# Ends of stages in a three-block fp32 network on one core: table loads ahead of waits, the second block's sum before the first's end, low parts by GpSimd

## The reference

```python
def _swiglu(t, w_gate, w_up, w_down):
    return (silu(t @ w_gate) * (t @ w_up)) @ w_down
# block 1, two layers
f = _swiglu(_rmsnorm(h, ffn1_pre_g[l]), ...)
h = h + 0.5 * _rmsnorm(f, ffn1_post_g[l])
u = _rmsnorm(h, mix_pre_g[l])            # -> three kinds of attention
h = h + _rmsnorm(merged @ w_out[l], mix_post_g[l])
f = _swiglu(_rmsnorm(h, ffn2_pre_g[l]), ...)
h = h + 0.5 * _rmsnorm(f, ffn2_post_g[l])
# stick-breaking attention, one of the three
log_beta = log_sigmoid(z); log_not = where(mask, log_beta - z, 0)
w = where(mask, exp(log_beta + reversed_cumsum(log_not) - log_not), 0)
# block 2, layers 0 and 1: ffn, mixer (sgu or rwkv), ffn
x = layer_norm(DN_ALPHA * x + 0.5 * swiglu(x, w_in, w_out), g, b)
x = layer_norm(DN_ALPHA * x + mix, g, b)
# block 3, one layer: attentions, convolution, hgrn; then
x = layer_norm_3(DEEPNORM_ALPHA * x + mixed, ln1_g, ln1_b)
ff = square(relu(x @ w_ff1)) @ w_ff2
```

## Time and profile before

| | us |
|---|---|
| median of three runs (lowest, highest) | 3549.11 (3548.95, 3560.91) |
| the profiled execution's own time | 3548.89 |
| its span in the trace | 3547.1 |
| PE busy | 3217.7 |
| DVE busy | 1777.1 |
| ACT busy | 1483.4 |
| POOL busy | 166.1 |
| mean granted TensorE clock, share of full | 0.92 |

### The profile page before, as it was taken

One profiled execution on the slowest core, in us unless ns is written; L12 is line 12 of the kernel. 1 busy time (PEld: TensorE's weight loads), 2 busy tenths in 40 slices (PEclk: granted clock), 3 DMA queues, 4 the chain that ended last, 5 costly groups with the idle time before them and its releaser, 6 DMA issues.

```text
span 3547.1 us, 54473 instructions
## 1 busy us (share of the span) xinstructions
PE 3217.7 (91%) x23904; PEld 2928.2 (83%) x23904; DVE 1777.1 (50%) x2137; ACT 1483.4 (42%) x1843; POOL 166.1 (5%) x210
## 2 busy tenths in 40 slices
PE   6999798999999798999998999998798998776798
PEld 6989787998988788989997898997597997655687
DVE  4554444545554435555543545446655543444655
ACT  4454734444454734444453344444303443321244
POOL 0000100000000100000000000000000000502100
PEclk9999888999999889999997999999798997867799
DMA  5543223554543224555551455553102453300253
GB/s 214 185 167 122 92 108 120 190 179 175 181 155 131 93 86 151 182 190 181 188 178 48 154 186 178 182 184 135 51 4 76 169 185 127 110 21 28 83 184 137
DMA packets 68591, 488.67 MB, mean 138 GB/s; under 512 B 7723, under 2 KB 9147, under 8 KB 9605
## 3 DMA queue, kind: packets, MB, share of 16 engines
q1 hardware_dynamic: 63936, 464.94, 36.8%
q10 hardware_dynamic: 4420, 20.26, 1.6%
HBM read 484.11 MB, written 1.06 MB: 137 GB/s over the span
## 4 chain that ended last, share of the span: by engine, by line
PE 79%; DVE 9%; ACT 8%; issue 2%; POOL 1%; PEld 1%; DMA 1%; DVEq 0%; ACTq 0%; PEldq 0%; SPq 0%; POOLq 0%
PE bank L100 52%; PE acc L100 26%; DVE weights_lo L315 2%; ACT weights_hi L110 2%; PEld acc L100 1%; ACT L1109 1%; ACT act_gate L640 1%; DVE h L652 1%; POOL hgrn_pairs_q L2913 0%; DVE h L663 0%; PE bank L683 0%; DVE xn L1670 0%; PE acc L968 0%; DVE b_x_lo L496 0%; ACT b_x_hi L110 0%
## 5 line engine op out<-in xcount | busy, mean ns | idle before, releaser
L315 DVE TENSOR_TENSOR weights_lo<-weight_ring,weights_hi 128x2048 fp32r<-128x2048 f32 x440 | 1009.8, 2295 | 1034.4 <-ACT weights_hi L110 1033.9
L100 PE MATMUL bank<-b_x_hi,weights_hi 128*128 128x256 f32 x3880 | 1102.9, 284 | 15.3 <-DVE weights_lo L315 6.4
L100 PE MATMUL bank<-b_x_hi,weights_lo 128*128 128x256 f32 x3880 | 1099.1, 283 | 0.0
L100 PE MATMUL bank<-b_x_lo,weights_hi 128*128 128x256 f32 x3880 | 1098.0, 283 | 0.0
L110 ACT ACTIVATE weights_hi<-weight_ring 128x2048 fp32r<-128x2048 f32 x440 | 839.6, 1908 | 436.9 <-PE acc L100 399.6
L100 PEld LDWEIGHTS bank<-b_x_hi,weights_hi 128*128 128x128 f32 x3880 | 739.2, 191 | 30.8 <-issue 15.5
L100 PEld LDWEIGHTS bank<-b_x_lo,weights_hi 128*128 128x128 f32 x3880 | 739.6, 191 | 3.2
L100 PEld LDWEIGHTS bank<-b_x_hi,weights_lo 128*128 128x128 f32 x3880 | 737.4, 190 | 0.0
L100 PE MATMUL acc<-weights_hi,b_hidden_hi 128*128 128x512 f32 x832 | 330.2, 397 | 0.0
L100 PE MATMUL acc<-weights_hi,b_hidden_lo 128*128 128x512 f32 x832 | 328.7, 395 | 0.0
L100 PE MATMUL acc<-weights_lo,b_hidden_hi 128*128 128x512 f32 x832 | 328.1, 394 | 0.0
(11 more groups left out here) (488 smaller groups left out, 4302.9 us busy)
## 6 DMA issues: line engine op xcount, KB each, us to landing
weight_ring<-in_weights SPq DMA_DIRECT2D x440, 1024.0 KB, 4.8
xn<-in_norm_rows ACTq DMA_DIRECT2D x15, 1024.0 KB, 4.7
bias_hankel<-bias_scratch ACTq DMA_DIRECT2D x1, 1536.0 KB, 6.2
cons<-in_shape_constants SPq DMA_DIRECT2D x1, 1408.0 KB, 6.8
h<-in_x SPq DMA_DIRECT2D x1, 1024.0 KB, 8.8
...
```

The costliest lines, as they stand in the source:

```text
L100: return pe.matmul(out, a, b, start=start, stop=stop, skip_group_check=True)
L315: dve.tensor_tensor(k.w.lo[:, n % 2, :], k.ring[:, n % RING, :], k.w.hi[:, n % 2, :], ALU.subtract) \
```

## The change

- `act_add_norm` and `act_residual` load the table with Sqrt first, ahead of their wait for the sum.
- In `act_add_norm` ACT squares the first half of block 1's sum without waiting for DVE's product by the gain; DVE waits for the squares instead.
- `dve_residual` does add 0, gain 0, add 1, norm 0, gain 1, norm 1; before, add 0, gain 0, norm 0, add 1, gain 1, norm 1.
- The low part of the unit behind an end is made by GpSimd (`pool_lo`), for 11 units: those behind `mixed` and `ffn2` of both layers, and the last units of f2(0,0), sgu, f2(0,2), f2(1,0), rwkv's output, f2(1,2) and block 3's output. Their mark is `w_lo_pool`, for which PE and SP wait. Behind `ffn1` DVE keeps it.
- `pe_features` runs a second warm behind `made` of block 1's first half in three places and none between the blocks; the transposes for `in2`, `h` "in" and `in3` stand ahead of their barriers, with 12 warm matmuls, each half with its own wait. `pe_h_features` is called for rwkv's output as well and gives it 12 warm matmuls too, where there were none.
- Scores of stick-breaking attention, the forget gates and hgrn load the set that holds Exp and Ln together ahead of their first wait. The compiled programs hold 114 table loads before and 85 now.

```diff
...
+EXP_AND_LN = "natural_log_exp_and_others"
...
 def unit(k, pe, *what, a=KT):
-    pe.wait_ge(*k.s.at("w_lo", n))
+    pe.wait_ge(*k.s.at(*low_mark(k, n)))
...
 def lo(k, dve):
+def lo_of_pool(k):
+    if k.s.counting:
+        k.by_pool.append(k.n_lo)
+    k.n_lo += 1
+def pool_lo(k, pool):
+    n = k.by_pool[k.n_pool]
+    k.n_pool += 1
+    pool.wait_ge(*k.s.at("w_hi", n))
+    pool.tensor_tensor(k.w.lo[:, n % 2, :], k.ring[:, n % RING, :], k.w.hi[:, n % 2, :], ALU.subtract) \
+        .then_inc(*k.s.up("w_lo_pool", n))
+def low_mark(k, n):
+    return ("w_lo_pool" if n in k.by_pool else "w_lo", n)
...
 def sp_weights(k, sp):
-            sp.wait_ge(*k.s.at("w_lo", n - RING))
+            sp.wait_ge(*k.s.at(*low_mark(k, n - RING)))
...
 def dve_units(k, dve, n):
+def dve_units_but_last(k, dve, n):
+    dve_units(k, dve, n - 1)
+    lo_of_pool(k)
...
 def act_add_norm(...):
+    act.preload_act_table(ACT.Sqrt)
...
+        first = 1 - b
...
-        act.activation(half(k.unread, 1), half(acc_of(k, b), 1), ACT.Square, accum_out=stat(k, 1, b)) \
-            .then_inc(*k.s.up("sq_sum", of, b, 1))
-        act.wait_ge(*k.s.at("sq_sum", of, b, 1))
-        act.activation(stat(k, 2, b), stat(k, 1, b), ACT.Identity, scale=s / D, bias=k.eps(s * 1e-6)) \
+        act.activation(half(k.unread, first), half(acc_of(k, b), first), ACT.Square, accum_out=stat(k, first, b)) \
+            .then_inc(*k.s.up("sq_sum", of, b, first))
+        act.wait_ge(*k.s.at("sq_sum", of, b, first))
+        act.activation(stat(k, 2, b), stat(k, first, b), ACT.Identity, scale=s / D, bias=k.eps(s * 1e-6)) \
...
-        act.wait_ge(*k.s.at("gained", of, b, 0))
-        act.activation(half(k.unread, 0), half(acc_of(k, b), 0), ACT.Square, accum_out=stat(k, 0, b)) \
-            .then_inc(*k.s.up("sq_sum", of, b, 0))
-        act.wait_ge(*k.s.at("sq_sum", of, b, 0))
-        act.activation(stat(k, 3, b), stat(k, 0, b), ACT.Sqrt, scale=s / D, bias=stat(k, 2, b)) \
+        if b == 0:
+            act.wait_ge(*k.s.at("gained", of, b, 0))
+        act.activation(half(k.unread, b), half(acc_of(k, b), b), ACT.Square, accum_out=stat(k, b, b)) \
+            .then_inc(*k.s.up("sq_sum", of, b, b))
+        act.wait_ge(*k.s.at("sq_sum", of, b, b))
+        act.activation(stat(k, 3, b), stat(k, b, b), ACT.Sqrt, scale=s / D, bias=stat(k, 2, b)) \
...
 def dve_add_norm(...):
-            if i:
-                dve.wait_ge(*k.s.at("sq_sum", of, b, 1))
+            if b + i:
+                dve.wait_ge(*k.s.at("sq_sum", of, b, i))
...
 def act_residual(k, act, of, scale):
+    act.preload_act_table(ACT.Sqrt)
...
 def dve_residual(...):
-    for b in range(NB):
+    def add(b):
...
-        dve.scalar_tensor_tensor(out=k.t[:, b], in0=h, scalar=stat(k, 1, b), in1=k.rows[:, 0], op0=ALU.add,
+    def gain(b):
+        dve.scalar_tensor_tensor(out=k.t[:, b], in0=k.h[:, b, :], scalar=stat(k, 1, b), in1=k.rows[:, 0], op0=ALU.add,
...
+    def norm(b):
...
-            dve.scalar_tensor_tensor(out=half(h, i), in0=half(k.t[:, b], i), scalar=stat(k, 6, b),
+            dve.scalar_tensor_tensor(out=half(k.h[:, b], i), in0=half(k.t[:, b], i), scalar=stat(k, 6, b),
...
+    add(0)
+    gain(0)
+    add(1)
+    norm(0)
+    gain(1)
+    norm(1)
...
-def pe_features(k, pe, of, src, taken, warm=0, at=2, made=True):
+def pe_features(k, pe, of, src, taken, warm=0, at=2, made=None, midway=None):
...
 def pe_features(...):
+    if midway:
+        pe.wait_ge(*k.s.at(*midway))
+        pe_warm(k, pe, warm, 0)
...
-            if made:
-                pe.wait_ge(*k.s.at("made", of, b, i))
+            pe.wait_ge(*k.s.at("made", made or of, b, i))
...
-        if b == 0:
-            pe_warm(k, pe, warm // 4, 0)
...
-def dve_ffn(k, dve, f):
+def dve_ffn(k, dve, f, next_by_pool=True):
...
-    lo(k, dve)
+    if next_by_pool:
+        lo_of_pool(k)
+    else:
+        lo(k, dve)
...
 def act_sb_scores(...):
+    act.preload_act_table_set(EXP_AND_LN)
...
 def act_forget(k, act, l):
+    act.preload_act_table_set(EXP_AND_LN)
...
 def pe_layer(k, pe, l):
-    pe_features(k, pe, ("pre1", l), k.t, in_parts(("pre1", l)), warm=12 * l)
+    pe_features(k, pe, ("pre1", l), k.t, in_parts(("pre1", l)), warm=12 * l,
+                midway=("made", ("ffn2", 0), 1, 0) if l else None)
...
-    pe_features(k, pe, ("pre2", l), k.t, in_parts(("pre2", l)), warm=12)
+    pe_features(k, pe, ("pre2", l), k.t, in_parts(("pre2", l)), warm=12, midway=("made", ("mixed", l), 1, 0))
...
 def dve_layer(k, dve, l):
-    dve_ffn(k, dve, ("ffn1", l))
+    dve_ffn(k, dve, ("ffn1", l), False)
...
-    dve_units(k, dve, 4)
+    dve_units_but_last(k, dve, 4)
...
 def pool_layer(k, pool, l):
+    pool_lo(k, pool)
+    pool_lo(k, pool)
...
 def pe_block1(k, pe):
+    pe_features(k, pe, ("in2",), k.h, in_parts(("in2",)), warm=12, made=("ffn2", 1))
...
 def dve_sgu(k, dve):
-    dve_units(k, dve, 8)
+    dve_units_but_last(k, dve, 8)
...
 def pe_h_features(k, pe, of, at):
-    pe_features(k, pe, ("h", of), k.h, lambda p: ("h_features", of, p), at=at, made=False)
+    pe_features(k, pe, ("h", of), k.h, lambda p: ("h_features", of, p), at=at, warm=12, made=("r2", 1, 0))
...
 def pe_rwkv_in(k, pe):
-    for i in range(2):
-        pe.wait_ge(*k.s.at("made", ("r2", 1, 0), 1, i))
-    pe_h_features(k, pe, "in", 4)
...
 def dve_rwkv_out(k, dve):
-    dve_units(k, dve, 4)
+    dve_units_but_last(k, dve, 4)
...
 def pool_rwkv_out(k, pool):
+    pool_lo(k, pool)
+    pool_lo(k, pool)
...
 def pe_block2(k, pe):
-    for b in range(NB):
-        for i in range(2):
-            pe.wait_ge(*k.s.at("made", ("ffn2", 1), b, i))
-    pe_features(k, pe, ("in2",), k.h, in_parts(("in2",)), made=False)
...
-    pe_warm(k, pe, 20, 0)
+    pe_h_features(k, pe, "in", 4)
...
-    pe_warm(k, pe, 20, 0)
+    pe_features(k, pe, ("in3",), k.h, in_parts(("in3",)), warm=12, made=("r2", 1, 2))
...
 def pool_block2(k, pool):
+    pool_lo(k, pool)
...
+    for _ in range(3):
+        pool_lo(k, pool)
...
 def act_hgrn(k, act):
+    act.preload_act_table_set(EXP_AND_LN)
...
 def pe_block3(k, pe):
-    for b in range(NB):
-        for i in range(2):
-            pe.wait_ge(*k.s.at("made", ("r2", 1, 2), b, i))
-    pe_features(k, pe, ("in3",), k.h, in_parts(("in3",)), made=False)
...
 def dve_block3(k, dve):
-    dve_units(k, dve, 4)
+    dve_units_but_last(k, dve, 4)
...
 def pool_block3(k, pool):
+    pool_lo(k, pool)
```

More of the change, by code:

```diff
@@ L83 @@
     tensor_copy = tensor_reduce = reciprocal = memset = dma_start = drain = wait_ge = then_inc = matmul
+    preload_act_table_set = preload_act_table = matmul
 class Pair:
@@ L232, in __init__ @@
         self.s = Signals(nc, ctx)
-        self.plan, self.unit_marks = [], []
+        self.plan, self.unit_marks, self.by_pool = [], [], []
         self.begin()
@@ L237, in begin @@
     def begin(self):
-        self.n_unit = self.n_hi = self.n_lo = 0
+        self.n_unit = self.n_hi = self.n_lo = self.n_pool = 0
         self.emptied = [()] * 8
```

## The result

The changed kernel takes 3499.74 us (median of four executions, 3498.02 to 3507.6), the kernel before beside it 3553.84 us; the ratio is 0.985 (95% interval 0.983 to 0.988), 1.5% less. A later set of four gives 3501.51 us and the same ratio (0.985, 0.982 to 0.988). The forecast was 3478.5 us, 2.0% less: the direction was right, and the gain was some 54 us between these medians where 70 were forecast.

A forecast was written before the change was run, and what follows sets the result against it. PE's products were taken as the floor, with some 330 us of PE idleness open to change; gains of 75.5 less costs of 5.1, net 70.4 from 3548.9, gave 3478.5 us, range 3460 to 3500.

The forecast's parts named there:

- attention: Stick-breaking attention: ACT sets the pace, fewer table loads save 3.85 us a pair, 32.9 us in two layers.
- Rival (a): PE bounds attention and the clock stays low, also at `ffn1`: 14.2 us less gain, about 3493 us; chance 0.22.
- rival (e): A table load costs more than its row, 5.9 us gained a pair instead of 3.85: 3462 us; chance 0.08.
- `ffn1`'s ends: Block 1's ends where DVE keeps the low part: root's load off the path, clock falls less; 3.0 each, 6.0 us.
- Normed ends: Ends behind `mixed` in two layers and `ffn2` in layer 0: next product at T + 12.0, 3.45 us each, 10.4.
- Residual ends: Ends by residual: early root load, DVE's new order, POOL's low part, transposes ahead of barriers; 21.6 us in all.
- (2) DVE beside POOL: Cost: DVE's `lo` or write may take longer while POOL moves the same memory; 0.8 us in all, between 0 and 4.
- POOL's low part itself: POOL's subtraction at 11 ends takes 5.2 us, is there at T + 4.4, needed at T + 10: costs nothing.
- (b): POOL's low part takes 11.5 us, 6.6 us more over 11 places: 3485 us; chance 0.12.
- (c): Slower than before: PE waits for POOL's low part at 11 ends, 3579 us if it takes 20 us; chance 0.02.
- Rwkv's warm matmuls: Cost at rwkv's output: 12 warm matmuls ahead of its transposes add 2.8 us.
- Clock behind the ends: Cost: ends without the three warm matmuls may begin some products at 1.2 GHz, +1.5 us.

The follow-up runs named there:

- `dve_all`: Changed kernel with all low parts made by DVE and none by POOL; 3493.07 us.
- `no_midway`: Changed kernel with all low parts by DVE, no second warm at three normed ends, no warm matmuls ahead of rwkv's output; one execution, 3485.06 us.
- the last version: Changed kernel with DVE's low parts, without second warm and rwkv's warm matmuls, same program as `no_midway`; 3486.70 us, ratio 0.981 to the kernel before.

## Why the prediction was wrong in its size

- **What bounds the kernel, and attention: right.** 32.9 us forecast (2 x 16.41 is 32.8), 31.0 found. ACT sets the pace at 12.5 us as worked out, and the clock rose with the shorter waits, as assumed. The windows of layer 0's phase, before and changed, have 0.92 and 0.98. Rival (a), PE at half clock, and rival (e), a load worth more than its row, would have shown 22 and 49 us; neither is seen.

```profile
324.98:435.04 110.06, 88.91 (x640) 84.10 (x638) 51.29 (x80) 76.50 (x91) 10.06 (x24) 0.92 0.31 112
```
```profile
321.68:416.25 94.57, 84.68 (x640) 79.94 (x638) 50.85 (x80) 57.48 (x76) 10.05 (x24) 0.98 0.35 123
```

- **`ffn1`'s ends: right**, 6.0 forecast, 5.5 found; PE's two waits there are 2.9 us instead of 4.1.

```profile
PE bank L101 <- DVE weights_lo L319: 2.9, 2, 1.7
```

- **Normed ends: 3.45 each forecast, 2.8 found; `in2` 3.35, found 1.7 to 1.9.** Layer 0's `ffn2` has its first product at T + 12.6 (791.42, with T = 778.80), not T + 12.0. Block 1's `h` (785.07 + 1.41 = T + 7.7) came later than T + 7.0, mostly since the write of block 0's `h` was longer beside POOL (1.0 us). That isn't all of the miss: with DVE's low parts (`dve_all`) the normed ends give 3.0 each and `in2` 0.6.
- **Residual ends: the step that failed.** Six ends were forecast to give 19.3 us; 5.9 and 7.1 were found. The step is "(2) DVE beside POOL: [...] 0.8 in all, between 0 and 4": the prediction took it that DVE goes on beside POOL, somewhat slower. Seven products by the gain alone grew by 16.2 us, and four writes of `h` by 1.0 each, 20.2 in all, 25 times the term. In the six ends the products' part is 14.0 us (16.2 less the 2.1 of `ln1_3`), and 19.3 - 14.0 = 5.3, near what was found. With DVE making the low part again the six ends give 17.1. So the new chain (add 0, gain 0, add 1, norm 0) was right in sum, though not end by end: "2a" gave 1.4 us where 4.3 were forecast, r2(0,2) 4.9 where 3.15 were. With the term as measured the whole sum is 70.4 + 0.8 - 16.2 - 4.0 = 51.0; the stretches of the table show 52.4, less 2.7 for rwkv's warm matmuls. That the two are so close is in part luck, since the sum has hgrn and the last two ends in it (`ln1_3` forecast 1.8 and found 0.3 longer than before, `ln2_3` 0.5 and 0.75), and not all of a longer row lies on the path. Hgrn's 1.3 us can't be told from the spread.
- **POOL's low part itself: right.** 5.2 us taken, 4.6 found, and no wait of PE ends with it. Rivals (b) and (c) asked how late POOL would be; the question was what POOL does to DVE meanwhile, and no rival did.
- **Rwkv's warm matmuls: right**, 2.8 forecast. From ACT's `head_numbers` to its copy of the projection's first unit it is 2.7 us more than before (2644.72 to 2666.83, 22.1 us; before 2681.61 to 2700.99, 19.4). Without them (`no_midway`) it is 19.4 again. Taking them out is part of the last version.
- **Clock behind the ends: right in sign at one kind, wrong at the other.** +1.5 was charged. Behind the three normed ends the clock is up throughout, where before it was at half for the transposes. At r2(0,0) it is lower than before (0.88, not 0.94) and comes up when DVE isn't held by POOL (1.00): there the longer product costs clock too. Beside the ends, rwkv's input projections lose up to 10 us in some executions and sgu 2.6, whatever the version. This is why the profiled execution of the changed kernel, 3507.6 us, stands 7 us above its others.
- **The base.** The three times of before had a median of 3549.11 us; over all of its executions it is about 3557. Both kernels are measured beside each other in the ratio, and by it the gain is 53 us. The range went from 3460 to 3500; 3499.74 lies just inside it and the later 3501.51 just outside. That owes something to luck: the upper part of the range was there for rival (a), which did not happen.
